# Gated delta-rule layer: the gate product of the output weights moves from GpSimd to VectorE

## The reference

```
mod = c_act @ ada_w[i] + ada_b[i]
shift, scale, gate = jnp.split(mod, 3, axis=-1)
h = rms_norm(x, norm_w[i]) * (1.0 + scale[:, None, :]) + shift[:, None, :]
y = gdn_mixer(h, ...)            # ends with  o.reshape(bsz, T, GDN_V) @ w_out
x = (x + gate[:, None, :] * y).astype(x.dtype)
return rms_norm(x, final_norm_w)
```

## Time and profile before

| | |
|---|---|
| time, median of 3 runs | 1169.2 us (1167.16 to 1170.16) |
| profiled execution, its own time | 1174.33 us |
| its span, first to last instruction | 1172.5 us |
| PE busy | 1080.8 us, 92% |
| VectorE busy | 840.6 us, 72% |
| ScalarE busy | 449.6 us, 38% |
| GpSimd busy | 595.9 us, 51% |
| mean granted TensorE clock | 0.975 |

### The profile page before, as it was taken

The page is one execution under the profiler, slowest core; times in us unless marked ns, Lnnn a source line. Parts: engine busy times, 40 slices in busy tenths (PEclk is TensorE's granted clock), DMA queues, the critical chain, the costliest instruction groups (busy, mean ns, idle before and its releaser), DMA issues.

```text
span 1172.5 us, 19022 instructions
## 1 busy us (share of the span) xinstructions
PE 1080.8 (92%) x5372; PEld 880.3 (75%) x5372; DVE 840.6 (72%) x1872; ACT 449.6 (38%) x1038; POOL 595.9 (51%) x819
## 2 busy tenths in 40 slices
PE   3896799989999999989999999999999999999984
PEld 2775687878878787878878787877878787887863
DVE  4777686876858586786858587685868777696845
ACT  4651433344243433434343433434343333434333
POOL 2344644575444844566445754456444853457513
PEclk9898899999999999999999899999999999999998
DMA  9922312213122321223121221213212132213012
GB/s 312 326 59 75 82 40 65 57 55 83 39 64 56 82 56 46 55 57 97 39 64 41 81 68 40 64 38 100 56 47 55 55 82 55 64 38 100 22 45 115
DMA packets 142049, 87.25 MB, mean 74 GB/s; under 512 B 21254, under 2 KB 136616, under 8 KB 141992
## 3 DMA queue, kind: packets, MB, share of 16 engines
q1 hardware_dynamic: 141992, 86.68, 26.5%
HBM read 77.76 MB, written 8.91 MB: 74 GB/s over the span
## 4 chain that ended last, share of the span: by engine, by line
PE 60%; DVE 22%; issue 11%; ACT 3%; DVEq 1%; POOL 1%; DMA 1%; SPq 0%; ACTq 0%; POOLq 0%
PE bank L408 27%; PE bank L510 12%; DVE work L934 8%; DVE y L967 3%; DVE work L951 3%; PE bank L554 2%; PE bank L542 2%; PE bank L546 2%; PE bank L564 2%; DVE work L931 2%; PE bank L567 2%; PE bank L423 2%; PE bank L592 2%; PE bank L456 1%; PE bank L430 1%
## 5 line engine op out<-in xcount | busy, mean ns | idle before, releaser
L1351 POOL TENSOR_TENSOR w_lo<-w_raw,w_hi 128x256 fp32r<-128x256 f32 x384 | 331.2, 893 | 244.3 <-ACT w_hi L689 244.3
L408 PE MATMUL bank<-h_hi,w_hi 128*128 128x512 f32 x760 | 327.5, 431 | 0.0
L408 PE MATMUL bank<-h_lo,w_hi 128*128 128x512 f32 x760 | 300.1, 395 | 0.0
L408 PE MATMUL bank<-h_hi,w_lo 128*128 128x512 f32 x760 | 203.6, 400 | 0.0
L934 DVE SCALAR_TENSOR_TENSOR work<-pre,cw,work 128x512 f32<-128x512 f32 x192 | 172.3, 898 | 14.1 <-DVE work L931 5.3
L408 PEld LDWEIGHTS bank<-h_hi,w_hi 128*128 128x128 f32 x760 | 144.1, 190 | 29.4 <-issue 0.5
L408 PEld LDWEIGHTS bank<-h_hi,w_lo 128*128 128x128 f32 x760 | 142.8, 188 | 30.3
L408 PEld LDWEIGHTS bank<-h_lo,w_hi 128*128 128x128 f32 x760 | 144.2, 190 | 27.4 <-issue 0.5
L1401 POOL TENSOR_TENSOR og_lo<-work,og_hi 128x256 fp32r<-128x256 f32 x64 | 47.2, 737 | 217.1 <-ACT og_hi L749 217.1
L715 ACT ACTIVATE work<-work 128x512 f32<-128x512 f32 x64 | 40.2, 628 | 264.8 <-DVE pre L942 127.7
L510 PE MATMUL bank<-wo_hi,og_hi 128*128 128x512 f32 x256 | 114.2, 446 | 7.2 <-DVE y L967 7.2
(11 more groups left out here) (177 smaller groups left out, 1815.3 us busy)
## 6 DMA issues: line engine op xcount, KB each, us to landing
w_raw<-in_gdn_w_in SPq DMA_DIRECT2D x96, 512.0 KB, 4.0
work<-in_ada_w SPq DMA_DIRECT2D x8, 1024.0 KB, 9.6
w_raw<-in_gdn_w_out SPq DMA_DIRECT2D x16, 512.0 KB, 3.3
y<-in_x SPq DMA_DIRECT2D x8, 512.0 KB, 9.1
work<-in_ada_w SPq DMA_DIRECT2D x8, 512.0 KB, 6.3
n_dram<-work SPq DMA_DIRECT2D x16, 256.0 KB, 3.6
out<-y SPq DMA_DIRECT2D x8, 512.0 KB, 2.6
work<-in_ada_b SPq DMA_DIRECT2D x1, 512.0 KB, 5.3
```

What stands on the lines that cost most here:

```text
L408: mm = nc.tensor.matmul(bank[m % 2][:, :], w[:, m % 2, k, :], h[:, k, half, :], start=(r == 0), stop=(r == MM - 1))
L1351: i = nc.gpsimd.tensor_tensor(w_lo[:, k % 2, j:j + 2, :], w_raw_k[:, k % 2, j:j + 2, :], w_hi[:, k % 2, j:j + 2, :].bitcast(F32), ALU.subt ...
```

## The change

`gate_wo` leaves GpSimd, where it was four instructions of 256 columns a tile, and becomes one VectorE instruction of 1024 columns a tile. On VectorE the product of wo0 stands behind k's convolution, that of wo1 behind `merge_d_out(u, 2)`. ScalarE, PE and SP keep their instructions and waits.

```diff
--- before.py
+++ after.py
@@ -1014,6 +1014,11 @@
+            def gate_wo(hd, i):
+                tile_landed(dve, hd, 0, f"wo{i}")
+                nc.vector.tensor_tensor(w_raw[:, 1 - i, :], w_raw[:, 1 - i, :], gate_bc[:, :], ALU.mult
+                                        ).then_inc(S["wo_gated"], 1)
+
             def attn(u):
@@ -1077,6 +1082,8 @@
                 merge_p_out(u, 0)
                 eps_of_q(u)
+                if first:
+                    dve.wait_ge(gate_done, 2)
                 if not first:
@@ -1087,6 +1094,8 @@
                 silu(u - 1, 5, cvv[:, 1, :])
                 if not last:
                     conv(u, par, nxt, 0)
+                if par == 0:
+                    gate_wo(hd, 0)
                 merge_d_out(u, 1)
@@ -1096,6 +1105,8 @@
                 if not last:
                     decay_k(u + 1, other)
                 merge_d_out(u, 2)
+                if par == 0:
+                    gate_wo(hd, 1)
                 if not last:
                     k_scalars(u + 1, other)
                     make_n(u + 1, other)
@@ -1359,13 +1370,6 @@
-            def gate_wo(hd, i):
-                tile_landed(pool, hd, 0, f"wo{i}")
-                for j in range(0, D_MODEL, 256):
-                    o = nc.gpsimd.tensor_tensor(w_raw[:, 1 - i, j:j + 256], w_raw[:, 1 - i, j:j + 256],
-                                                gate_bc[:, j:j + 256], ALU.mult)
-                o.then_inc(S["wo_gated"], 1)
-
@@ -1416,15 +1420,11 @@
                 if not last:
                     if first:
                         split_lo(u, 2)
-                        pool.wait_ge(gate_done, 2)
                     mask_g(u + 1)
-                    if par == 0:
-                        gate_wo(hd, 0)
                     if not first:
                         split_lo(u, 2)
                     if par == 0:
                         split_wo(hd, 0)
-                        gate_wo(hd, 1)
                     norm_k(u + 1)
                     mask_decay(u + 1)
                     if par == 0:
```

## The result

The changed kernel takes 1174.34 us (median of 8 runs, 1172.38 to 1176.67), the kernel before 1168.32 us in the same number of runs. The ratio is 1.0053, 95% interval 1.0037 to 1.0068: slower by 6.0 us. The sign was right; the forecast of 1189 us and its range from 1178 were too high. The profiled execution of the changed kernel took 1176.15 us with a span of 1174.4.

What follows compares the result with a forecast made beforehand. PE, 92% busy, was taken to be bound by its waits for VectorE's SiLU of k ahead of `turn_k`. Terms 2.7 + 7 x (1.3 + 0.35) + 5.9 = +20.1 us on 1169.2 gave 1189 us, range 1178 to 1197.

Steps and rivals of the forecast that it cites:

- The bound: Ahead of `turn_k`: PE waits most for VectorE's SiLU of k, line 951, 16 times, 31.6 us together.
- The price of the instruction: One two-input VectorE product of 1024 columns: 1.2 us, low end 1.0, high end 1.48 beside GpSimd.
- The lengthening of the chain: Behind k's convolution: product 1.2 us plus ScalarE's rounding 1.0 us ahead of k's tanh, 2.2 us in all.
- The relief: VectorE's v and k work without GpSimd's wo0 product beside it: 0.75 + 0.35 - 0.2, some 0.9 us.
- the sum at `turn_k`: Chain growth less relief, 2.2 - 0.9 = +1.3 us in each of units 2 to 14.
- The 0.75 for v's taps and SiLU: VectorE's SiLU of v and last two taps of v get quicker without GpSimd's wo0 product, 0.75 us.
- The - 0.2 for GpSimd's tail in the new product: GpSimd's split reaches 0.3 us into VectorE's new wo0 product; 0.2 us taken off the gain.
- clock term: Gap at `turn_k` grows to 4.0 us, all seven of units 2 to 14 fall: +5.9 us, bounds 0 and +10.4.
- the sign of being wrong: Waits for line 951 staying under 3 us, or PE making up for them in the chunk loop.
- The second product: wo1's product behind the last merge delays `scale_v` past ScalarE's 1.7 us slack: +0.35 us in units 2 to 14.
- Unit 0: `turn_k` +0.7 us and +2.0 us from wo1's product by way of `scale_v`, together +2.7 us.
- The second rival: Each GpSimd product holds VectorE off for its whole 3.28 us; about 1156 us, faster; decides above 2.2 us; chance 0.04.

Runs made afterwards that it cites:

- tanh first: Changed kernel with ScalarE's rounding of wo0 put behind k's tanh; ratio 0.9939 to the kernel before.
- the last experiment: Kernel before, both products still on GpSimd, wo0's moved behind split_lo(u, 2), ScalarE's tanh ahead of the rounding; ratio 1.0075 to the kernel before.

## Why the prediction was wrong

- **The bound was read rightly.** The wait ahead of `turn_k` is on the path: taking 1.0 us out of it (tanh first) or 1.8 us (product left out) shortened the kernel by that in every even unit and by the clock's falls.
- **The price of the instruction** was taken at 1.2 us; measured 1.21 at the median of 16, 1.49 at most beside GpSimd. The 1.48 us read from the earlier trace rows as the price beside GpSimd is a mean: three of those seven instructions ran with GpSimd idle, at 1.3 us, the other four beside it at 1.7.
- **The lengthening of the chain**, 1.2 + 1.0 = 2.2 us, measured 2.0 us. Right.
- **The relief was the step that failed**: "Net relief 0.75 + 0.35 - 0.2, some 0.9 us." Measured in unit 4, from the first merge's start (373.47 before, 376.88 after) to the end of k's convolution, it is 1.86 us, and 0.33 us more in k's SiLU: 2.2 us in all, so the sum at `turn_k` is -0.2 and not +1.3 us. The 0.75 for v's taps and SiLU was right. What was left out, by its rows: the short copy that closes v's convolution took 0.70 us beside GpSimd's product and 0.16 without, and k's SiLU took 0.80 us against 1.13. The second of these does not come from the missing product (with it left out altogether SiLU still took 1.13) but from the later place of SiLU beside GpSimd's splits. What was too small: k's taps gained 0.59, not 0.35 us. The - 0.2 for GpSimd's tail in the new product did not show: GpSimd's split ran beside all of the product, which took 1.22 us, and it was the split that got longer, 4.93 against 4.16 us. Experiment: 1.8 us of relief with the product left out, and a kernel with only wo0 moved at 1.0014. Over units 2 to 14, 7 x 1.3 = 9.1 us were put down for `turn_k` and -0.5 measured: 9.6 of the 14 us too many hang on this step directly, and the clock term with it.
- **The clock term**, +5.9 us, rested on the gap growing to 4.0 us. It stayed at 2.6 us, under the 3 us that the prediction gave as the sign of being wrong, and the falls stayed as many (4 of 7, against 5). Its premise was gone; whether 4.0 us would have cost what was put down for it, no run here tried.
- **The second product** was forecast at +0.35 us in each of units 2 to 14 by way of `scale_v`, measured as a wait of 0.38 us and 0.3 to 0.5 us of length. Right, though the starts written there, 402.85 and 402.56, give 0.29. Unit 0: waits of 3.5 to 4 us at line 542 were forecast, 3.86 measured; its `turn_k` stands 6.66 us behind the start of k's convolution as before (125.01 - 118.35, 125.14 - 118.48), not 0.7 us more, and the fall of the clock behind the longer wait, 2.7 us, was not foreseen: the prediction counted falls at `turn_k` only.
- **The sign was in part luck.** The forecast had 15 of its 20 us at `turn_k` in units 2 to 14 and in the clock behind it, and nothing of the slowdown came from there. What made the kernel slower were the smaller terms: unit 0 and the second product.
- **The odd units** got 1.7 us shorter in all by the gap on VectorE described above, which no term of the forecast had.
- **The second rival** ("the relief is the full GpSimd time", 3.28 us, decided above 2.2) got 0.04. The relief reached 2.2 us, just the point from which it would have decided. The Trainium skill's "SBUF — State Buffer", section "Summary: rules for kernel authors", lets the one of the two that is issued second wait for the whole of the first, where VectorE's has two SBUF inputs and GpSimd's reads SBUF. The trace agrees more than the prediction allowed: v's taps, its SiLU and k's taps, all with two inputs, got shorter. The copy got shorter most in proportion (0.70 to 0.16 us) and has only one input; the second copy right behind it took 0.16 us beside the same product before the change. And with the product left out 1.8 of 3.28 us came back, not all.

## What to carry to other kernels

When work leaves an engine beside which the instructions of the bottleneck's feeder run longer, as VectorE's did here beside GpSimd, list every instruction of the feeder that overlapped it, short copies too, and what each takes without it; the prediction's list gave 0.9 of 1.9 us. Before an operation is put into a chain, look at what stands ahead of the chain's next link on the other engines: here one rounding in front of a tanh that did not need it was worth 13 us, more than the change itself. Slack is used up by order, not by busy time: GpSimd at 51% could not take its own product 7 us later.

## What the runs showed of the hardware beyond that

- With GpSimd's product of wo0 ahead of it, k's three taps take 3.05 or 3.62 us beside the same GpSimd split, with the two starts 0.04 or 0.05 us apart in either case. Both occur in one execution: of units 2 to 14 six took the longer time and one the shorter in the kernel before, two and five with only wo1's product moved. What decides between them is open.
- A semaphore raised by VectorE's queue came 0.41 or 0.42 us before the end of the copy ahead of it, in each of units 2 to 14.
- Waits of 2.6 to 2.8 us ahead of `turn_k` were followed by a fall of the clock in 4 or 5 of units 2 to 14 in every such kernel, waits of 1.9 to 2.2 us in some, waits of 1.6 us and less in none. The waits of 2.6 us at line 542 in the last experiment were followed by one in two of seven.
